# Input projections of a hybrid trunk: three bf16 products in place of one fp32 product, the low halves kept in the weights' own words

## The chip, the cores and the metric

One core of one Trainium2 chip. The metric is the device time of one execution in microseconds (us). The engines of the core are TensorE (PE, matrix products, with a sequencer for weight loads shown as PEld), VectorE (DVE), ScalarE (ACT), GpSimd (POOL) and SyncE (SP), which here issues nearly all DMA transfers. Each engine works through its own list of instructions in order; semaphores hold one back for another.

## What is computed

Two layers of a trunk over 256 latent and 256 context tokens of width 1024. Cut to what matters here:

```python
for layer in range(DEPTH):                      # DEPTH = 2
    h = rmsnorm(x, g) * (1 + m[1]) + m[0]       # latent and context tokens: 512 rows of 1024
    p = h @ w_in[layer]                         # 1024 x 3840, the input projections
    # columns of p: A q,k,v (512 + 256) | B q,i,f_fwd,f_bwd,g (5 x 512) | C q,k,v (512)
    a = diff_attention(p[A]); b = hgrn2(p[B]); c = windowed_attention(p[C])
    x = x + m[2] * (concat(a, b, c) @ w_out[layer])
    x = x + m[5] * ffn(rmsnorm(x) ...)          # layer 0: dense SwiGLU, layer 1: top-2-of-8 experts
```

Inputs, weights and output are fp32. Layer 1 needs no new context tokens, so its queries and gates are computed for the latent tokens alone.

## The kernel before

**Stages.** Per layer: norm of the tokens (into `HT`, 1024 features on 8 x 128 partitions, 512 tokens); input projections; turning of queries and keys (`pe_qkt`); attention (`pe_att`, `act_att`, `dve_att`); the levels of HGRN2 (`pe_levels`), its states, the output projection; then the FFN (layer 0) or the experts (layer 1). The FFN, the output projection and the experts already split each fp32 operand into a bf16 high and low half and add three bf16 products; the input projections multiply fp32 by fp32.

**The projections** (`proj_units`, `pe_proj_mm`) come in eight groups of columns, in this order: `aqk` (queries and keys of A), `c` (all of C), `bff` and `bfb` (the forget gates), `bq`, `av`, `bi`, `bg`. A group has 4 units, a unit is 8 matmuls, one for each block `k` of 128 features, added up in one PSUM bank. For `bff`, `bfb` and `bq` (kind "T") the weights are the stationary operand and up to 512 tokens stream past (in layer 1 `bq` takes 256); for the others (kind "N") 128 tokens are stationary and 512 columns of weights stream (`av` 256). `bg` has 4 units in layer 0 and 2 in layer 1. The trace gives each fp32 matmul as two records.

**The order on PE.** `pe_proj_first` issues the first six groups. In layer 0 pieces of another product (the modulation, `pe_ada_mm`, and its spreading, `pe_ada_spread`, which waits for small copies of the DVE) stand between them. Then `pe_qkt`, the first unit of `bi`, and the attention, between whose steps `pe_proj_fill` puts the other units of `bi` (24 matmuls in layer 0, 16 in layer 1). What is left, `bg` and in layer 1 the last unit of `bi`, is filled into the levels.

**The order on DVE.** `dve_proj_first` copies the units of `aqk` and `c` out of PSUM (L784), then `dve_qk` norms queries and keys (L813 to L832). In its middle GpSimd computes a power (`pool_qk`, L840 and L841), for which the DVE waits (L820); after it GpSimd rotates the latent queries and keys (L855 to L861). In layer 1 16 gate operations (`dve_gates`) follow, which wait for ACT's last sigmoid of `bfb`; in both, the copies of `av`, then those of `pe_qkt` (L1217), then the attention. ACT takes `bff`, `bfb`, `bq`, `bi` and `bg` out of PSUM.

**The attention** runs in steps `s`, one for a head and 128 queries; each passes from PE (scores) to DVE (maximum), ACT (exponential), DVE (ratio), PE (transposes), ACT (copy), PE (product) and DVE (output).

**The weights** are loaded by SP into two rings, R0 and R1, of 16 KiB per partition, groups in turn: `aqk`, `bff`, `bq`, `bi` into R0; `c`, `bfb`, `av`, `bg` into R1. A load starts when PE has done the last unit of the group before in that ring.

```python
def raw_full(eng, key):          # waits until the group's load has landed
    it = items[key]
    eng.wait_ge(S(f"ring_full_{it['place']}"), it["full"])
    return it["raw"]
```

## Time and profile before

| | |
|---|---|
| median of 3 runs | 1839.96 us (1839.65 to 1841.42) |
| the profiled execution | span 1838.2 us from its first to its last instruction; no other time is listed for it |
| PE busy | 1769.7 us (96%), 14950 matmul records |
| DVE busy | 1151.5 us (63%) |
| ACT, POOL busy | 368.6 us (20%), 82.9 us (5%) |
| mean granted clock of TensorE | 0.998 of 2.4 GHz |
| HBM | 221 GB/s over the span; above 400 GB/s in the last third (the experts) |

Such shares don't say where a change pays: they are means over stages with different limits. The rows below are therefore taken from the chain of waits and from the timelines of single stretches. Times in them count from the start of the span. A granted clock of 1.00 is 2.4 GHz, of 0.50 1.2 GHz.

### The profile page before, as it was taken

Reading aid. Unit: us, or ns where it says so; the run is one execution under the profiler, and the core shown is the slowest. Engines: PE = TensorE matmul, PEld = TensorE weight load, DVE = VectorE, ACT = ScalarE, POOL = GpSimd, SP = SyncE. Lnnn points to the kernel's source line nnn. Section 1 sums busy time; section 2 is a strip of 40 time slices with the busy share of each in tenths; the row PEclk is TensorE's granted clock in tenths of the full one; section 3 lists DMA queues with packets and bytes.
Section 4 is the critical chain, followed back from the end, with each engine's and each line's share of the span. In section 5 each row is a group of like instructions: output and inputs, shape, how many; then the busy total and the mean of one; then the engine's idle time right before and its main releaser. Section 6 shows DMA issues by size and latency. Waiting matters only on the chain.

```text
span 1838.2 us, 34033 instructions
## 1 busy us (share of the span) xinstructions
PE 1769.7 (96%) x14950; PEld 1114.3 (61%) x15001; DVE 1151.5 (63%) x1385; ACT 368.6 (20%) x671; POOL 82.9 (5%) x76
## 2 busy tenths in 40 slices
PE   6999999989999999999999978999999999999998
PEld 2434556674544444445465644878696878778695
DVE  1240176896433323214224696999999999999998
ACT  1101155242422222112013432201101010000000
POOL 0033000020000000000330001000000000000000
PEclk9999999999999999999999999999999999999999
DMA  9832200002445454230221017699999999999994
GB/s 371 309 138 69 92 1 29 18 24 98 174 188 206 183 206 160 94 113 3 89 92 69 1 47 281 255 417 409 418 416 415 418 412 419 413 418 410 412 416 194
DMA packets 98842, 408.72 MB, mean 222 GB/s; under 512 B 14008, under 2 KB 20856, under 8 KB 84368
## 3 DMA queue, kind: packets, MB, share of 16 engines
q1 hardware_dynamic: 96504, 405.54, 56.0%
q8 instruction: 119, 1.95, 0.4%
q10 hardware_dynamic: 2200, 1.08, 0.2%
q14 instruction: 19, 0.16, 0.0%
HBM read 405.55 MB, written 1.05 MB: 221 GB/s over the span
## 4 chain that ended last, share of the span: by engine, by line
PE 79%; DVE 10%; DMA 4%; issue 3%; ACT 2%; PEld 1%; ACTq 0%; PEldq 0%; DVEq 0%; SPq 0%; POOL 0%; POOLq 0%
PE PS L1548 12%; PE PS L1924 10%; PE PS L710 9%; PE PS L708 8%; PE PS L1506 6%; PE PS L1898 5%; PE PS L1900 5%; PE PS L1901 5%; DMA ARENA<-in_moe_w 3%; DVE ARENA L2020 2%; PE PS L454 2%; PE PS L1412 2%; PE PS L1274 2%; DVE ARENA L908 2%; DVE ARENA L905 1%
## 5 line engine op out<-in xcount | busy, mean ns | idle before, releaser
L2020 DVE TENSOR_TENSOR ARENA<-ARENA 128x2816 bf16<-128x2816 f32 (+2 forms) x184 | 567.3, 3122 | 23.1 <-DMA ARENA<-in_moe_w 22.6
L1898 PE MATMUL PS<-ARENA 128*128 128x96 bf16 x2816 | 378.6, 209 | 5.8 <-DVE ARENA L2020 3.0
L1900 PE MATMUL PS<-ARENA 128*128 128x96 bf16 x2816 | 378.4, 209 | 1.7 <-issue 1.7
L1901 PE MATMUL PS<-ARENA 128*128 128x96 bf16 x2816 | 378.3, 206 | 0.4 <-issue 0.2
L1900 PEld LDWEIGHTS PS<-ARENA 128*128 128x128 bf16 x2816 | 354.7, 126 | 8.8 <-issue 8.6
L1898 PEld LDWEIGHTS PS<-ARENA 128*128 128x128 bf16 x2816 | 346.3, 123 | 11.8 <-issue 7.5
L1901 PEld LDWEIGHTS PS<-ARENA 128*128 128x128 bf16 x2816 | 298.4, 106 | 2.5 <-issue 2.4
L710 PE MATMUL PS<-ARENA 128*128 128x512 f32 (+1 forms) x608 | 236.9, 530 | 1.3 <-DVE ARENA L623 1.3
L1924 PE MATMUL PS<-ARENA 128*96 128x512 bf16 x960 | 216.1, 384 | 0.4 <-DVE ARENA L2020 0.4
L1548 PE MATMUL PS<-ARENA 128*128 128x512 bf16 x960 | 213.5, 379 | 1.7 <-issue 0.6
L1924 PEld LDWEIGHTS PS<-ARENA 128*96 128x96 bf16 x960 | 116.2, 122 | 93.7 <-issue 0.8
L1548 PEld LDWEIGHTS PS<-ARENA 128*128 128x128 bf16 x984 | 95.0, 98 | 124.8 <-issue 11.7
L710 PEld LDWEIGHTS PS<-ARENA 128*128 128x128 f32 x608 | 109.4, 190 | 85.1 <-issue 79.8
L708 PE MATMUL PS<-ARENA 128*128 128x512 f32 (+1 forms) x384 | 153.7, 559 | 0.0
L387 DVE TENSOR_TENSOR ARENA<-ARENA 128x4096 bf16<-128x4096 f32 (+1 forms) x26 | 91.5, 3519 | 80.9 <-ACT ARENA L381 80.8
L708 PEld LDWEIGHTS PS<-ARENA 128*128 128x128 f32 x384 | 72.2, 190 | 80.7 <-issue 79.1
L1506 PE MATMUL PS<-ARENA 128*128 128x512 bf16 x517 | 113.5, 379 | 1.5 <-DVE ARENA L1600 0.9
L1600 DVE TENSOR_TENSOR ARENA<-PS,ARENA 128x512 f32<-128x512 f32 x22 | 15.2, 692 | 140.7 <-PE PS L1548 140.7
L381 ACT ACTIVATE ARENA<-ARENA 128x4096 bf16<-128x4096 f32 (+1 forms) x26 | 75.1, 2890 | 90.5 <-PE PS L1506 68.3
L1506 PEld LDWEIGHTS PS<-ARENA 128*128 128x128 bf16 x528 | 51.6, 98 | 63.5 <-issue 1.4
L784 DVE COPY ARENA<-PS 128x512 f32<-128x512 f32 (+1 forms) x24 | 13.4, 557 | 107.1 <-PE PS L710 107.1
L1988 ACT ACTIVATE ARENA<-PS 128x384 f32<-128x384 f32 (+1 forms) x48 | 20.7, 465 | 276.1 <-PE PS L1901 275.3
(242 smaller groups left out, 1704.4 us busy)
## 6 DMA issues: line engine op xcount, KB each, us to landing
ARENA<-in_moe_w SPq DMA_DIRECT2D x128, 1408.0 KB, 13.9
ARENA<-in_moe_w SPq DMA_DIRECT2D x48, 1536.0 KB, 16.0
ARENA<-in_ada_w SPq DMA_DIRECT2D x24, 2048.0 KB, 10.1
ARENA<-in_ffn_w SPq DMA_DIRECT2D x15, 2048.0 KB, 7.8
ARENA<-in_w_in SPq DMA_DIRECT2D x11, 2048.0 KB, 7.9
ARENA<-in_moe_w SPq DMA_DIRECT2D x16, 1024.0 KB, 16.0
ARENA<-in_w_in SPq DMA_DIRECT2D x6, 1024.0 KB, 7.0
ARENA<-in_w_out SPq DMA_DIRECT2D x8, 512.0 KB, 4.5
```

The lines of the kernel that those rows point to most:

```text
L381: act.activation(it["hi"], raw, ACT.Copy).then_inc(S("split_hi"), 1)
L387: dve.tensor_tensor(it["lo"], it["raw"], it["hi"], ALU.subtract).then_inc(S("split_lo"), 1)
L454: mm = pe.matmul(ps[32 * g:32 * g + 32, :], SC[:, 2 * kk + n, :], w[:, n, 512 * g:512 * g + 512], start=kk == 0 and n == 0, stop=kk == 3 a ...
L708: mm = pe.matmul(B(bank)[:, part], slot[:, k, P * u:P * u + P], HT[:, k, part], start=k == 0, stop=k == KC - 1)
L710: mm = pe.matmul(B(bank)[:, part], HT[:, k, P * u:P * u + P], slot[:, k, part], start=k == 0, stop=k == KC - 1)
L1506: mm = pe.matmul(B(2 * x + h), a[:, c, P * x:P * x + P], w[:, at:at + 512], start=c == 0 and n == 0, stop=c == FC - 1 and n == 2)
L1548: mm = pe.matmul(B(b0 + i % 3), w[:, k, P * c:P * c + P], x[:, k, :], start=k == 0 and w is hi and x is HTH, stop=k == KC - 1 and w is lo)
L1898: pe.matmul(out, hi[:, h][:, f], HEH[:, k, :], start=k == 0 and b % 4 == 0, stop=False, skip_group_check=True)
L1900: pe.matmul(out, hi[:, h][:, f], HEL[:, k, :], start=False, stop=False, skip_group_check=True)
L1901: mm = pe.matmul(out, lo[:, h][:, f], HEH[:, k, :], start=False, stop=k == KC - 1, skip_group_check=True)
L1924: mm = pe.matmul(B(YBANK + h)[0:SLOTS, :], x, y[:, at:at + 512], start=c == 0 and n == 0, stop=c == FC - 1 and n == 2)
L2020: dve.tensor_tensor(WLO[q % NSLOT][:, 0:n], RAW[q % NSLOT][:, 0:n], WHI[q % NSLOT][:, 0:n], ALU.subtract).then_inc(S("m_lo"), 1)
```

## The change

All groups but `aqk` and `c` are computed as three bf16 products. The high half of an fp32 number is here the upper 16 bits of its word, read in place as bf16 with a step of two elements. The low half of a weight, the number less its high half, rounded to bf16, is written by the DVE over the lower 16 bits of the same word (`dve_proj_halve`), so that no further buffer is needed: one subtraction per group over 8 x 512 elements per partition (8 x 256 for `av`). The tokens' low half goes into a buffer of its own, `HTV` (`dve_tokens_low`), at the place of `G`, whose parts are written when the token tile that lies there has been used for the last time. PE waits for the subtraction of a group (`pe_proj_ready`) and no longer for its load. To make room, ring E1 and the small table `LAMV` move; two step counters of the DVE become one.

```diff
+        HTU = A(0, 2 * KC * 256).bitcast(BF16).rearrange("p (k n two) -> p k n two", k=KC, two=2)[:, :, :, 1]
+        HTV = A(80, KC * 256).bitcast(BF16).rearrange("p (u k t) -> p k u t", k=KC, t=P)
...
+        HALVED = ("bff", "bfb", "bq", "av", "bi", "bg")
+        def word_halves(v):
+            v = v.rearrange("p k n -> p (k n)").bitcast(BF16).rearrange("p (k n two) -> p k n two", k=KC, two=2)
+            return v[:, :, :, 1], v[:, :, :, 0]
...
+        def dve_proj_halve(dve, L, key):
+            raw, w = raw_full(dve, (key, L)), 256 if key == "av" else 512
+            hi, lo = word_halves(raw)
+            dve.tensor_tensor(lo[:, :, 0:w], raw[:, :, 0:w], hi[:, :, 0:w], ALU.subtract).then_inc(S("proj_halved"), 1)
+        def dve_tokens_low(dve, L):
+            dve.wait_ge(S("norm_ht_act"), 16 * L + 8)
+            dve.wait_ge(S("norm_ht_dve"), 16 * L + 8)
+            high, full = (v.rearrange("p k (u t) -> p k u t", t=P) for v in (HTU, HT))
+            dve.tensor_tensor(HTV, full, high, ALU.subtract).then_inc(S("proj_halved"), 1)
+        def pe_proj_ready(pe, L, key):
+            if key not in HALVED:
+                raw_full(pe, (key, L))
+                return
+            pe.wait_ge(S("proj_halved"), proj_halved(L, key))
...
-            if kind == "T":
+            if key in HALVED:
+                hi, lo = word_halves(slot)
+                out = B(bank)[:, part]
+                if kind == "T":
+                    tiles_of = slice(part.start // P, part.stop // P)
+                    terms = [(hi, HTU[:, k, part], out),
+                             (hi, HTV[:, k, tiles_of, :], out.rearrange("p (u t) -> p u t", t=P)),
+                             (lo, HTU[:, k, part], out)]
+                    terms = [(o, w[:, k, P * u:P * u + P], x) for w, x, o in terms]
+                else:
+                    terms = [(out, x, w[:, k, part])
+                             for x, w in ((HTU[:, k, P * u:P * u + P], hi), (HTV[:, k, u, :], hi),
+                                          (HTU[:, k, P * u:P * u + P], lo))]
+                for m, (o, x, y) in enumerate(terms):
+                    mm = pe.matmul(o, x, y, start=k == 0 and m == 0, stop=k == KC - 1 and m == 2)
+            elif kind == "T":
...
                 dve_proj_one(dve, L, n)
+                if n == 3:
+                    dve_tokens_low(dve, L)
+                if n == 5:
+                    dve_proj_halve(dve, L, "bff")
             dve_qk(dve, L)
+            dve_proj_halve(dve, L, "bfb")
+            dve_proj_halve(dve, L, "bq")
             if L > 0:
                 dve_gates(dve, L)
...
+            dve_proj_halve(dve, L, "av")
             for n in range(5 * NT, 6 * NT):
                 dve_proj_one(dve, L, n)
+            dve_proj_halve(dve, L, "bi")
...
             for s in range(len(us) + 4):
+                if s == 6:
+                    dve_proj_halve(dve, L, "bg")
```

The DVE's list around the norm in layer 0, from the copies of `c`'s last two units (L784; L498 and L502 are copies of the modulation) to the first of `pe_qkt`. Before:

```order
L784 COPY ARENA<-PS 128x512
L813 TENSOR_TENSOR ARENA<-ARENA 128x2048
...
L828 TENSOR_TENSOR ARENA<-ARENA,QKG 128x4x256 x2
L832 TENSOR_TENSOR ARENA<-ARENA,SQKG 128x4x256
L832 TENSOR_TENSOR ARENA<-ARENA,SQKG 128x4x128
L502 COPY MT<-PS 128x16
L498 COPY GATE<-PS 128x512 x4
L509 SCALAR_TENSOR_TENSOR MT<-MT,VECS 128x16
L784 COPY ARENA<-PS 128x256 x4
L1217 COPY ARENA<-PS 128x512 x3
```

With the change (L831 is the copy, L720 a group's subtraction):

```order
L831 COPY ARENA<-PS 128x512
L868 TENSOR_TENSOR ARENA<-ARENA 128x2048
...
L887 TENSOR_TENSOR ARENA<-ARENA,SQKG 128x4x128
L720 TENSOR_TENSOR ARENA<-ARENA 128x4096 x2
L505 COPY MT<-PS 128x16
L501 COPY GATE<-PS 128x512 x4
L512 SCALAR_TENSOR_TENSOR MT<-MT,VECS 128x16
L720 TENSOR_TENSOR ARENA<-ARENA 128x8x256
L831 COPY ARENA<-PS 128x256 x4
L720 TENSOR_TENSOR ARENA<-ARENA 128x4096
L1272 COPY ARENA<-PS 128x512 x3
```

The subtractions of `bfb` and `bq` come behind the whole norm, that of `bi` behind the copies of `av` and ahead of those of the turned queries and keys.

In the attention's seventh step, the DVE's list with the change (L1405 ends a step's ratio, L1374 writes an output, L1381 is a maximum):

```order
L1398 RECIPROCAL ARENA<-ARENA 128x2
L1401 TENSOR_SCALAR ARENA<-ARENA,LAM 128x1
L1405 SCALAR_TENSOR_TENSOR ARENA<-ARENA 128x256
L720 TENSOR_TENSOR ARENA<-ARENA 128x4096
L1374 TENSOR_SCALAR ARENA<-PS,ARENA 128x64
L1381 TENSOR_REDUCE ARENA<-PS 128x2
L1384 TENSOR_SCALAR ARENA<-ARENA 128x2
```

There the subtraction of `bg` stands between two steps that before followed each other directly.

## Rows read from the trace of the kernel before

**Rows 1.** The page, the chain that ended last: shares by engine and by line
```profile
PE 79%; DVE 10%; DMA 4%; issue 3%; ACT 2%; PEld 1%; ACTq 0%; PEldq 0%; DVEq 0%; SPq 0%; POOL 0%; POOLq 0%
...
PE PS L1548 12%; PE PS L1924 10%; PE PS L710 9%; PE PS L708 8%; PE PS L1506 6%; PE PS L1898 5%; PE PS L1900 5%; PE PS L1901 5%; DMA ARENA<-in_moe_w 3%; DVE ARENA L2020 2%; PE PS L454 2%; PE PS L1412 2%; PE PS L1274 2%; DVE ARENA L908 2%; DVE ARENA L905 1%
```

**Rows 2.** The chain in order of time: start, length (us), engine, tile, line
```profile
91.14 1.05 PE PS L489 x2
...
109.25 7.06 PE PS L708 x16
...
136.01 34.53 PE PS L708 x80
...
203.89 13.83 PE PS L710 x64
...
221.67 6.87 PE PS L710 x16
...
321.40 1.72 PE PS L710 x4
...
472.56 10.77 PE PS L1480 x96
...
891.86 68.75 PE PS L708 x192
...
960.61 13.83 PE PS L710 x64
...
1047.79 1.72 PE PS L710 x4
```

**Rows 3.** Busy time by stretch, a piece of the FFN in bf16
```profile
core 0: us, PE busy (x) PEld busy (x) DVE busy (x) ACT busy (x) POOL busy (x), PEclk, DMA share, GB/s
506.39:517.13 10.74, 10.74 (x49) 4.88 (x50) 3.60 (x6) 2.82 (x3) 0.00 (x0) 1.00 0.69 280
```

**Rows 4.** Instruction groups, first 760 us: the FFN subtractions on DVE
```profile
L387 DVE TENSOR_TENSOR ARENA<-ARENA 128x4096 bf16<-128x4096 f32 x13 | 57.5, 4422 | 30.4 <-ACT ARENA L381 30.4
...
L387 DVE TENSOR_TENSOR ARENA<-ARENA 128x2048 bf16<-128x2048 f32 x6 | 13.7, 2287 | 1.7 <-ACT ARENA L381 1.6
```

**Rows 5.** Timeline of DVE, both layers: start, length, operation [idle before, releaser]
```profile
86.85 0.69 DVE L784 COPY ARENA<-PS 128x512 f32<-128x512 f32 x1 [8.23 <-PE PS L710]
...
130.57 2.29 DVE L820 TENSOR_TENSOR ARENA<-ARENA,STAT 128x2048 f32<-128x2048 f32 x1 [15.43 <-POOL STAT L841]
...
137.05 1.82 DVE L832 TENSOR_TENSOR ARENA<-ARENA,SQKG 128x1024 f32<-128x1024 f32 x2
...
922.47 1.82 DVE L832 TENSOR_TENSOR ARENA<-ARENA,SQKG 128x1024 f32<-128x1024 f32 x2
```

**Rows 6.** The page, DMA issues of the projections' weights: KB, us to landing
```profile
ARENA<-in_w_in SPq DMA_DIRECT2D x11, 2048.0 KB, 7.9
```

**Rows 7.** Timeline of PE behind two idle times
```profile
22.80 3.14 PE L454 MATMUL PS<-ARENA,SC 128*32 128x512 f32 x16 [3.04 <-DMA ARENA<-in_ada_w]
...
1142.41 1.45 PE L1670 MATMUL PS<-K,ARENA 128*128 128x128 f32 x8 [2.08 <-DVE ARENA L671]
```

**Rows 8.** Busy time by stretch: clock, attention, levels, rotation, gates
```profile
22.80:27.00 4.20, 4.20 (x22) 1.64 (x23) 0.00 (x0) 0.00 (x0) 0.00 (x0) 0.59 1.01 420
...
1142.40:1147.00 4.60, 4.59 (x18) 1.86 (x18) 1.63 (x3) 1.33 (x3) 0.00 (x0) 0.63 1.01 415
...
138.90:153.50 14.60, 14.60 (x35) 6.46 (x34) 0.00 (x0) 2.66 (x5) 13.96 (x16) 1.00 0.41 144
...
228.50:262.20 33.70, 32.85 (x155) 18.40 (x154) 23.76 (x89) 20.09 (x73) 0.00 (x0) 1.00 0.00 0
...
339.50:388.00 48.50, 42.74 (x229) 28.30 (x228) 48.50 (x126) 16.74 (x26) 0.00 (x0) 1.00 0.00 1
...
946.80:960.60 13.80, 13.80 (x65) 12.15 (x65) 6.91 (x16) 3.52 (x6) 0.00 (x0) 1.00 0.24 76
```

**Rows 9.** Instruction groups, first 760 us: weight loads, fp32 and bf16
```profile
L1548 PEld LDWEIGHTS PS<-ARENA 128*128 128x128 bf16 x984 | 95.0, 98 | 124.8 <-issue 11.7 <-DVE ARENA L1600 1.5
...
L710 PEld LDWEIGHTS PS<-ARENA 128*128 128x128 f32 x320 | 57.0, 190 | 53.4 <-issue 51.4 <-ACT ARENA L555 0.2 <-DVE ARENA L623 0.2
```

More of the change, by code:

```diff
@@ L207, in trunk @@
         SQX = [A(108, NT, D), A(93, NT, D), A(93, NT, D), A(20, NT, D)]
-        LAMV = A(68, DEPTH, 4, 32)
+        LAMV = A(128, DEPTH, 4, 32)
         ROWS = A(57, P)
@@ L247, in since @@
             return L * in_layer0[name]
-        RAW_AT = {"R0": A(129, KC, 512), "R1": A(145, KC, 512), "E0": A(40, KC, 512), "E1": A(72, KC, 512),
+        RAW_AT = {"R0": A(129, KC, 512), "R1": A(145, KC, 512), "E0": A(40, KC, 512), "E1": A(64, KC, 512),
                   "E2": A(24, KC, 512),
@@ L400, in trunk @@
         ENG = ("pe", "act", "dve", "pool")
+        dve_steps = [0]
         stage_count = {e: 0 for e in ENG}
@@ L701, in proj_part, with proj_halved @@
             return slice(256, 512) if late else slice(0, 512 if key in ("bff", "bfb", "bq") else w)
+        HALVED = ("bff", "bfb", "bq", "av", "bi", "bg")
+        def word_halves(v):
+            v = v.rearrange("p k n -> p (k n)").bitcast(BF16).rearrange("p (k n two) -> p k n two", k=KC, two=2)
+            return v[:, :, :, 1], v[:, :, :, 0]
+        def proj_halved(L, key):
+            return (len(HALVED) + 1) * L + HALVED.index(key) + 2
+        def dve_proj_halve(dve, L, key):
[12 more added lines that the diff above has]
+            pe.wait_ge(S("proj_halved"), proj_halved(L, key))
         def pe_proj_mm(pe, L, n, k):
@@ L716, in pe_proj_first @@
                 if u == 0 and n + L > 0:
-                    raw_full(pe, (key, L))
+                    pe_proj_ready(pe, L, key)
                 banks = 4 if eng == "act" else 3
@@ L750, in pe_proj_fill @@
                 if key == "bi" and u == 0 or key == "bg" and u == proj_units(L)[-1][1] - (NT if L == 0 else 2) + 1:
-                    raw_full(pe, (key, L))
+                    pe_proj_ready(pe, L, key)
                 if j == 1:
@@ L1708, in dve_route @@
         def dve_route(dve):
-            step = [0]
             def then(ins):
-                step[0] += 1
-                ins.then_inc(S("r_step"), 1)
-                dve.wait_ge(S("r_step"), step[0])
+                dve_steps[0] += 1
+                ins.then_inc(S("dve_step"), 1)
+                dve.wait_ge(S("dve_step"), dve_steps[0])
             def low_rows(j):
@@ L2102, in dve_setup @@
         def dve_setup(dve):
-            step = [0]
             def then(ins):
-                step[0] += 1
-                ins.then_inc(S("setup_step"), 1)
-                dve.wait_ge(S("setup_step"), step[0])
+                dve_steps[0] += 1
+                ins.then_inc(S("dve_step"), 1)
+                dve.wait_ge(S("dve_step"), dve_steps[0])
             dve.wait_ge(S("vecs_copied"), 1)
```

## The prediction

> **What bounds the kernel now.** The page comes first. TensorE (PE) stands for 79% of the chain that ended last, and the projections' two lines, L710 and L708, are 17% of that chain [rows 1]. So the product that the change makes cheaper lies on the path. The chain in order of time then tells where: from 109 us to 229 us in layer 0, and from 892 us to 985 us in layer 1, it consists almost only of projection matmuls, end to end [rows 2]. Next, what a product costs. One fp32 matmul of the program is two records, so 80 records in 34.53 us are 40 matmuls of 0.863 us [rows 2]. A bf16 matmul of 512 columns is read from the FFN: 50 weight loads in 10.74 us, 0.215 us each (49 of the 50 matmul records are there) [rows 3]. At 256 columns it is 13.83 us for 32 fp32 matmuls, 0.432 us each [rows 2], against 96 bf16 ones of the FFN in 10.77 us, 0.112 us each [rows 2].
>
> The DVE's timeline is the last view, since the change gives the DVE seven long subtractions per layer and it works strictly in order. It stands still for 15.43 us in each layer in the middle of the queries' and keys' norm, waiting for GpSimd's power, and only after that does it finish the norm, at 138.9 us in layer 0 and 924.3 us in layer 1 [rows 5].
>
> **The change, step by step.** Three products cost 3 x 0.215 = 0.644 us for 0.863 us: 0.219 us saved per 512-wide matmul, so a unit of 8 takes 5.16 us for 6.91. A 256-wide group of 32 takes 10.8 us for 13.8. If everything stood on the path, layer 0 (160 wide matmuls, 32 narrow) would save 38 us and layer 1 (64 + 32 + 16 = 112 wide, 64 narrow) 31 us. The ceiling is 69 us. The rest of the working says why I take little of it.
>
> A subtraction of 4096 elements per partition takes 4.42 us, one of 2048 elements 2.29 us [rows 4]. The rows are for dense operands; the new ones step over 4 bytes and write half words, which no row shows. I take the dense price, since fp32 words are read in both, and keep twice the price as the far end.
>
> *Layer 0, to the start of attention (228.5 us before).* The tokens' low half fits between two of the DVE's copies, where 8.23 us stood idle [rows 5]. The halving of bff begins behind the copy at 86.85 us (0.69 long) and ends at 92.0; a small copy that followed at once before now comes behind it, and PE, which spread the first gate at 91.1 [rows 2] and must wait for that copy, comes 1.1 us later. Group bff starts at 110.35 and holds three ada chunks, (136.01 - 109.25 - 3 x 7.06) / 3 = 1.86 each: 3 x (7.06 - 1.75) + 3 x 1.86 + 5.16 = 26.7, end at 137.0. But bfb may not start before its own halving, which the program puts behind the whole norm: norm done at 138.9 + 1.1 = 140.0, halving to 144.5. **PE stands still 7.5 us.** Then bfb 20.6, bq 203.9 - 170.5 - 7.0 = 26.4 (its old stretch less the saving), av 10.8. The halvings of bq and av are hidden (bq is loaded 8 us after bff ends [rows 6], and the DVE is free). The halving of bi stands behind av's copies: +0.5, +4.4, and only then bi's first unit, 5.2; the turning of queries and keys (3.25 us) passes beside it. Without clock effects 212.4.
>
> The idle time costs clock. After 3.04 us of idle TensorE was granted 0.59 over 4.2 us, after 2.08 us 0.63 over 4.6 us [rows 7, 8]: most of each stretch at 1.2 GHz in place of 2.4, and 0.41 x 4.2 or 0.37 x 4.6 = 1.7 us of full-rate work lost each time. So the 7.5 us stall brings 1.7 us more: 214.1. **Saved: 14.4 us.**
>
> *Attention, layer 0.* 24 matmuls of bi lie between its steps. In the first 33.7 us PE is busy 32.85 [rows 8], which speaks for all of 24 x 0.219 = 5.3 us; but each step also passes through ACT and DVE in turn, the DVE being busy 23.8 of 33.7, so I take half, 2.6 (ends 0 and 5.3). Against it the halving of bg stands inside this loop at its seventh step. The DVE idles 33.7 - 23.8 = 9.9 us in some 17 steps there, 0.6 us a step, and wins back a part of that: +4.0 of the 4.42. PE then waits over 3 us, and loses clock again; here some of it is covered, +1.5 (ends 0 and 1.7). **Net +2.9.**
>
> *Levels, layer 0.* The first pieces of fill are on the chain, 2 matmuls in 1.72 us and then 2 more [rows 2]: 4 matmuls x 0.219 = **-0.9**. Later the DVE is busy 48.5 of 48.5 us [rows 8], so bg's other 28 matmuls save nothing.
>
> *Layer 1, to the start of attention (985.1 before).* The tokens' half and bff's halving are hidden: the copies there stand 3.5 to 6.9 us apart, a 256-wide unit or a 512-wide one in fp32, and PE has three banks for these units, so a copy that comes 1 us late holds nobody. Group bff runs from 891.9 to 912.5. The norm ends at 924.3, bfb's halving at 928.8: **PE stands still 16.3 us**, over twice what bff had saved, plus 1.7 for the clock. bfb to 951.1, bq (256 wide) to 961.9. The DVE's gates follow bfb and ACT's last two sigmoids (1.2 us): 6.9 us [rows 8], from 952.3 to 959.2; av's halving to 961.5, just in time. av to 972.7, copy and bi's halving to 977.6, bi's unit to 982.9. **Saved: 2.2.**
>
> *Attention and levels, layer 1.* 16 matmuls, 3.5 us at most, I take 2.0; halving of bg +4.0, clock +1.5: **+3.5**. Of the levels three matmuls lie on the chain, 2 of them in the row at 1047.79 [rows 2]: **-0.65**.
>
> What was in step behind each layer keeps its length: the FFN's loads and the experts' weights are started by events that all move together.
>
> Sum: -14.4 + 2.9 - 0.9 - 2.2 + 3.5 - 0.65 = -11.8 us. The profiled span of 1838.2 becomes 1826.4. The median of the runs, 1839.96, lies 1.8 above the span; I add that: **1828.2 us**. About 57 of the 69 us are lost, the larger part to waits for the DVE's halvings.
>
> **A rule that speaks against the change.** During bfb's and bq's halvings GpSimd rotates queries and keys: it was busy 13.96 of 14.6 us right where the DVE did nothing at all (0.00) [rows 8], so no row shows the two at work together. If they take turns at memory, bfb's halving takes up to 8.8 us, 4.4 us more on the path in each layer, and the sum is -3.0. The Trainium skill ("GPSIMD Engine Reference", the table of its properties) says that GpSimd's SBUF interfaces are shared with VectorE, with contention when a DVE instruction has two SBUF inputs, which these have. By that rule the gain would be the 3.0. The trace can't decide it. I keep it as a rival.
>
> **The rivals.**
> - *A: as worked out*, 1828.2. Chance 0.57.
> - *B: the short stalls don't cost clock, or the attention takes up more of the shorter fill.* For it: 2.08 us is the shortest idle time with a fallen clock in the rows, and the attention's stalls may be shorter or covered. Against it: the two long ones are well above. Without all four clock terms 6.4 us less: 1821.8; with all of the fills' 8.8 us in place of 4.6, 1817.6. Chance 0.15.
> - *C: DVE and GpSimd take turns*, 1828.2 + 8.8 = 1837.0, which is 0.16% under before: not to be told from no change, as a measurement of this kernel tells about 0.2%, 3.7 us. Chance 0.15.
> - *D: slower, by weight loads that step over 4 bytes.* The fp32 weight load takes 190 ns, the dense bf16 one 98 [rows 9]. Behind 215 ns of a 512-wide matmul either is hidden; behind the 112 ns of a 256-wide one the longer is not. All 96 products of bq in layer 1 and two of three of av in both layers load from fp32 words: 224 loads. At 190 ns for the 112 of the forecast that is +0.078 x 224 = +17.5 us, 1845.7. It decides against the change from 0.112 + 11.8 / 224 = 0.165 us per load. Against it: an fp32 matmul record of 512 columns lasts 0.43 us, twice a bf16 one, so an fp32 record may hold two rounds, its load too, and 190 be 2 x 95. Chance 0.08.
> - *E: slower, by halvings at twice the price.* Three per layer lie open (bfb, bi, bg), each +4.4: +26.5, 1854.7. Chance 0.05; a read and a write per clock don't depend on the step in any row here, but none has this step.
>
> **The numbers.** The likeliest gives 1828.2. The range, 1818 to 1841, holds A, B and C and the spread of the half-known terms (the fills' 4.2 us below, 3 us of load and queue times above), and leaves out D and E. Faster by over 0.2% are A, B and some of C: 0.76; within 0.2%: most of C, 0.13; slower: D and E, 0.11.
>
> **What would show it.** In the profile after: a 512-wide unit of 24 products in 5.16 us; PE idle 7 to 8 us before bfb in layer 0 and about 16 us in layer 1, both released by the DVE's subtraction; clock near 0.6 behind them; a subtraction of 4.42 us inside attention with PE idle after it; attention starting near 214 and, counted from bff's first matmul of layer 1, 91 us later for 93.3. Subtractions longer than 4.5 us beside GpSimd's rotation mean C, everywhere mean E; 256-wide groups above 12 us mean D. The forecast is wrong in kind if PE doesn't wait before bfb.

## The result: slower by 0.4%, and the profile after

| | before | with the change |
|---|---|---|
| median of 5 runs of each | 1839.96 us (1839.65 to 1842.61) | 1847.57 us (1847.30 to 1849.32) |
| ratio | | 1.0038, 95% interval 1.0025 to 1.0050 |
| profiled span | 1838.2 us | 1845.8 us |
| mean granted clock | 0.998 | 0.981 |

The forecast was 1828.2 us, faster. The time lies above its whole range. TensorE does have less to do, and yet the kernel takes longer. The page of the changed kernel, busy times, granted clock in 40 slices of 46 us, and the chain that ended last:

```profile
PE 1729.5 (94%) x15284; PEld 1096.5 (59%) x15369; DVE 1215.2 (66%) x1399; ACT 368.8 (20%) x671; POOL 101.2 (5%) x76
...
PEclk9999959999999999999989999999999999999999
...
PE 71%; DVE 13%; issue 4%; PEld 4%; DMA 3%; POOL 2%; ACT 1%; PEldq 0%; ACTq 0%; SPq 0%; DVEq 0%; POOLq 0%
```

PE is busy 1729.5 us, where it was 1769.7. The sixth slice, from 231 to 277 us, stands at 5 in the clock row. That is the attention of layer 0, where the forecast saw next to nothing. Against [rows 1] the DVE's share of the chain has grown from 10% to 13%, and PE's has fallen from 79% to 71%.

PE's timeline of the changed kernel at the places that the forecast named (start, length, operation, and in brackets the idle time before it and what ended that):

```profile
111.20 5.27 PE L753 MATMUL PS<-ARENA 128*128 128x512 bf16 x23 [0.17 <-issue]
...
118.25 5.51 PE L753 MATMUL PS<-ARENA 128*128 128x512 bf16 x23
...
145.30 3.59 PE L753 MATMUL PS<-ARENA 128*128 128x512 bf16 x8 [6.95 <-DVE ARENA L720]
...
235.45 1.09 PE L1329 MATMUL PS<-ARENA 128*128 128x64 f32 x4 [3.45 <-DVE ARENA L1374]
...
895.76 21.27 PE L753 MATMUL PS<-ARENA 128*128 128x512 bf16 x94
932.78 2.31 PE L753 MATMUL PS<-ARENA 128*128 128x512 bf16 x5 [15.75 <-DVE ARENA L720]
...
979.34 3.25 PE L1261 MATMUL PS<-K,ARENA 128*128 128x128 f32 x28 [0.61 <-DVE ARENA L831]
984.50 5.34 PE L753 MATMUL PS<-ARENA 128*128 128x512 bf16 x23 [1.91 <-DVE ARENA L720]
989.77 1.13 PE L1299 MATMUL PS<-ARENA 32*128 32x512 f32 x4
...
1013.98 1.94 PE L1329 MATMUL PS<-ARENA 128*128 128x64 f32 x8 [3.61 <-DVE ARENA L1374]
```

From one unit of `bff` to the next, 111.20 to 118.25, is 7.05 us, of which 1.86 are the modulation's piece: a unit takes 5.19 us, as forecast (5.16). PE waits 6.95 us before `bfb` in layer 0 and 15.75 us in layer 1 for a halving (L720); 7.5 and 16.3 were forecast. The wait of 3.45 us inside attention is also there. What is new stands in the clock. Busy time and granted clock by stretch, behind the two waits before `bfb` and then behind the two inside the attentions:

```profile
core 0: us, PE busy (x) PEld busy (x) DVE busy (x) ACT busy (x) POOL busy (x), PEclk, DMA share, GB/s
145.30:149.50 4.20, 3.97 (x9) 1.45 (x11) 2.92 (x1) 0.00 (x0) 4.12 (x4) 0.50 0.05 20
932.70:940.00 7.30, 7.00 (x20) 2.67 (x22) 5.48 (x2) 0.00 (x0) 7.26 (x3) 0.60 0.00 0
235.40:272.00 36.60, 35.88 (x114) 21.98 (x117) 18.57 (x67) 14.00 (x51) 0.00 (x0) 0.50 0.00 1
1013.90:1020.00 6.10, 6.02 (x17) 3.60 (x18) 3.14 (x10) 2.27 (x7) 0.00 (x0) 0.50 0.00 0
```

Behind the long waits in front of `bfb` TensorE is back at 2.4 GHz after 4 to 7 us. Behind the short one of 3.45 us in layer 0's attention it stays at 1.2 GHz for 36.6 us, although it is busy 98% of them. In layer 1, behind a wait of 3.61 us, it is back after some 6 us in this execution.

The DVE's timeline, with [rows 5] for comparison:

```profile
87.67 5.07 DVE L720 TENSOR_TENSOR ARENA<-ARENA 128x4096 bf16<-128x4096 f32 x1
92.59 0.20 DVE L505 COPY MT<-PS 128x16 f32<-128x16 f32 x1
...
140.56 4.68 DVE L720 TENSOR_TENSOR ARENA<-ARENA 128x4096 bf16<-128x4096 f32 x1
...
212.04 1.92 DVE L1272 COPY ARENA<-PS 128x512 f32<-128x512 f32 x3
218.50 0.69 DVE L1381 TENSOR_REDUCE ARENA<-PS 128x2 f32<-128x512 f32 x1 [4.55 <-PE PS L1299]
...
230.13 5.00 DVE L720 TENSOR_TENSOR ARENA<-ARENA 128x4096 bf16<-128x4096 f32 x1
```

A halving of 4096 elements takes 5.0 to 5.1 us and not 4.42 in two of these three rows; the one of `bfb`, with GpSimd's rotation beside it, takes 4.68. And between the copies of the turned queries and keys and the attention's first maximum the DVE stands idle for 4.55 us, 12 us before it is made to do the halving of `bg` in the middle of the attention.

Stage by stage, from the first instruction of one to that of the next (in us; differences are taken before rounding):

| | before | after | difference | forecast |
|---|---|---|---|---|
| start to attention, layer 0 | 228.5 | 217.8 | -10.7 | -14.4 |
| attention, layer 0 | 89.1 | 104.8 | **+15.6** | +2.9 |
| its end to `bff` of layer 1 | 574.1 | 573.2 | -0.9 | -0.9 |
| `bff` to attention, layer 1 | 93.4 | 94.0 | +0.6 | -2.2 |
| attention, layer 1 | 58.1 | 62.7 | +4.7 | +3.5 |
| its end to the end | 795.0 | 793.3 | -1.7 | -0.65 |
| sum | 1838.2 | 1845.8 | +7.6 | -11.8 |

Two thirds of the error of 19.4 us, 12.7 us, lie in one row.

### The profile page after: what moved, and what is told of

Read it like the earlier page. It is cut to its first block, busy times and chain, and to the rows that moved or that the text cites. A ratio compares the mean times of both kernels' runs of the same rounds, so it can differ in the third digit from the quotient of the medians.

```text
span 1845.8 us, 34751 instructions
## 1 busy us (share of the span) xinstructions
PE 1729.5 (94%) x15284; PEld 1096.5 (59%) x15369; DVE 1215.2 (66%) x1399; ACT 368.8 (20%) x671; POOL 101.2 (5%) x76
## 4 chain that ended last, share of the span: by engine, by line
PE 71%; DVE 13%; issue 4%; PEld 4%; DMA 3%; POOL 2%; ACT 1%; PEldq 0%; ACTq 0%; SPq 0%; DVEq 0%; POOLq 0%
PE PS L1605 12%; PE PS L1980 9%; PE PS L753 8%; PE PS L1563 6%; PE PS L1956 5%; PE PS L1954 5%; PE PS L1957 4%; PE PS L757 4%; PE PS L1469 2%; PE PS L1329 2%; PE PS L457 2%; DVE ARENA L720 2%; DVE ARENA L2076 2%; DMA ARENA<-in_moe_w 2%; DVE ARENA L963 2%
## 5 line engine op out<-in xcount | busy, mean ns | idle before, releaser
L1956 PEld LDWEIGHTS PS<-ARENA 128*128 128x128 bf16 x2816 | 354.7, 126 | 8.9 <-issue 8.9
L1954 PEld LDWEIGHTS PS<-ARENA 128*128 128x128 bf16 x2816 | 346.3, 123 | 12.2 <-issue 9.5
L1957 PEld LDWEIGHTS PS<-ARENA 128*128 128x128 bf16 x2816 | 298.5, 106 | 2.3 <-issue 2.2
L753 PE MATMUL PS<-ARENA 128*128 128x512 bf16 (+1 forms) x1068 | 230.2, 365 | 30.1 <-DVE ARENA L720 26.4
L753 PEld LDWEIGHTS PS<-ARENA 128*128 128x128 bf16 x1104 | 106.2, 99 | 140.3 <-DVE ARENA L720 27.6
L1605 PEld LDWEIGHTS PS<-ARENA 128*128 128x128 bf16 x984 | 95.0, 98 | 124.8 <-issue 11.7
L757 PE MATMUL PS<-ARENA 128*128 128x512 f32 (+1 forms) x256 | 99.4, 543 | 1.3 <-DVE ARENA L626 1.3
L1563 PEld LDWEIGHTS PS<-ARENA 128*128 128x128 bf16 x528 | 51.6, 98 | 63.5 <-issue 1.4
L757 PEld LDWEIGHTS PS<-ARENA 128*128 128x128 f32 x256 | 47.6, 190 | 50.2 <-issue 48.1
L1017 PE MATMUL PS<-ARENA 128*128 128x128 f32 x336 | 46.8, 290 | 21.0 <-ACT ARENA L988 14.2
```

The costliest lines, as they stand in the source:

```text
L753: mm = pe.matmul(o, x, y, start=k == 0 and m == 0, stop=k == KC - 1 and m == 2)
L757: mm = pe.matmul(B(bank)[:, part], HT[:, k, P * u:P * u + P], slot[:, k, part], start=k == 0, stop=k == KC - 1)
L1017: mm = pe.matmul(bank[:, c], KEX[:, h, c], crossed_queries(h, x, LEVELS[n_level]), start=True, stop=True)
L1563: mm = pe.matmul(B(2 * x + h), a[:, c, P * x:P * x + P], w[:, at:at + 512], start=c == 0 and n == 0, stop=c == FC - 1 and n == 2)
L1605: mm = pe.matmul(B(b0 + i % 3), w[:, k, P * c:P * c + P], x[:, k, :], start=k == 0 and w is hi and x is HTH, stop=k == KC - 1 and w is lo)
L1954: pe.matmul(out, hi[:, h][:, f], HEH[:, k, :], start=k == 0 and b % 4 == 0, stop=False, skip_group_check=True)
```

## The experiments

All times are medians, and each ratio is to the kernel before, measured beside that kernel on the same chip (1840.4 to 1842.0 us). Where no other kernel is named, a diff is against the change.

**Is it the halving of `bg` inside attention?** Two kernels take it out of its place: one leaves `bg` as one fp32 product, the other puts it 16 steps later in layer 0.

```diff
-        HALVED = ("bff", "bfb", "bq", "av", "bi", "bg")
+        HALVED = ("bff", "bfb", "bq", "av", "bi")
...
-                if s == 6:
-                    dve_proj_halve(dve, L, "bg")
```

> The changed kernel with group bg left in fp32, so that no halving stands inside the attention. Theory 1 (the halving in the attention lets TensorE's clock fall, and in the part with the context's queries it does not come back): the clock stays at 1.00 through both attentions, layer 0's attention takes about 86 us in place of 104, layer 1's about 55 in place of 62; about 0.9 + 0.65 us are given back in the levels. About 23 us less than the change, some 1824 us. Theory 2 (the attention is slow because its fill is now three short bf16 products): attention 0 stays near 100 us and the clock low, 1842 us or more.

Measured: 1824.02 us, ratio 0.991 (0.9893 to 0.9926). The attention takes 86.5 us in layer 0 and 55.8 in layer 1, with the clock at 1.00 in both. So one halving per layer, which saves 1.5 us of fill, costs 23.6 us.

```diff
-                if s == 6:
+                if s == (22 if L == 0 else 6):
```

> The changed kernel with the halving of bg in layer 0 at step 22 of the attention, in the part with the latent tokens' queries, in place of step 6. Theory 1 with the place as a cause (there 512-wide scores keep TensorE busier and the clock comes back within some 5 us, as in layer 1): attention 0 takes about 92 us in place of 104, some 1836 us. If any stall in this attention kept the clock low to its end: 100 us or more, 1845 us.

Measured: 1848.31 us (1839.54 to 1861.32), ratio 1.0035. The wait went along: PE stands still for 3.35 us at 273 us, the clock is 0.50 from there to 297 us, and the attention takes 100.8 us. The place inside the attention does not matter much; that it is inside does. Nor is the 6 us return of layer 1 to be relied on. This kernel has layer 1 as the change has it, and there PE waited 3.46 us; the clock was 0.50 up to 1027 us, and the attention took 68.2 us for 62.7:

```profile
1008.50:1020.00 11.50, 11.49 (x37) 7.43 (x38) 5.14 (x13) 3.87 (x10) 0.00 (x0) 0.50 0.01 1
```

**Is it the wait, or what the wait does to the clock?** Two kernels: the change with 16 useless bf16 matmuls for PE in the wait, and the kernel before with a useless subtraction of the tokens' low half (4.42 us, result not read) in the same seventh step.

```diff
+                    if s == 6:
+                        pe.wait_ge(S("proj_act"), since(L, "proj_act") + 3 * NT + 1)
+                        pe_keep_busy(pe, FILL_BANKS[0], 16)
                     pe.wait_ge(S(n + "at"), since(L, n + "at") + u + 1)
```

> The changed kernel with 16 matmuls without use, 512 columns of bf16 each (3.4 us at full clock), issued by PE in both attentions at the point where it waits for the DVE behind the halving of bg. The stall itself stays. Theory 1: the clock stays at 1.00 behind it, attention 0 falls from 104 us to about 91, attention 1 from 62 to about 60; some 1832 us. Rival (the stall costs by what queues up behind it on the DVE, not by the clock): no change, 1847 us.

Measured: 1845.88 us, ratio 1.0020, but spread from 1830.21 to 1856.98 over ten executions. The profiled one (1835.75) kept the clock at 1.00 in both attentions, and that of layer 0 took 90.7 us. Against the 86.5 us without a halving in it, the wait alone thus costs about 4 us there; the rest of the change's 104.8 us comes with the clock. Over all ten the time goes with the mean clock: 1830.21 us at 0.991, 1844.74 at 0.983, 1856.98 at 0.976. The filler was right where it was looked at, and no cure: what follows a wait in this attention differs from execution to execution.

```diff
+                if s == 6:
+                    high, full = (v.rearrange("p k (u t) -> p k u t", t=P) for v in (HTU, HT))
+                    dve.tensor_tensor(HTV, full, high, ALU.subtract).then_inc(S("stalled"), 1)
```

> The kernel before, with one subtraction without use of 4096 elements (4.42 us) put into the DVE's list at step 6 of both attentions; the products all stay fp32, and with them the fill between the steps. If the stall alone takes the clock down and the context part's small matmuls can't bring it back, whatever the fill: clock 0.50 for over 30 us, attention 0 about 14 us longer, attention 1 about 5 us, 1859 us. If the longer fp32 fill holds the clock or brings it back within 5 us: attention 0 about 5 us longer, 1849 us.

Measured: 1854.02 us, ratio 1.0070 (1.0053 to 1.0087); four executions from 1852.4 to 1854.3 at a mean clock of 0.994 to 0.995, and the profiled one 1874.2 at 0.982. Its two lines of attention in layer 0:

```profile
240.00:250.00 10.00, 7.38 (x30) 4.38 (x29) 8.76 (x21) 3.79 (x16) 0.00 (x0) 0.81 0.00 0
250.00:297.50 47.50, 47.50 (x130) 26.89 (x129) 21.93 (x74) 17.04 (x58) 0.00 (x0) 0.50 0.00 1
```

Not one product was changed here, and a PE wait of 2.62 us was followed by over 47 us at 1.2 GHz with PE busy throughout. So the fall needs no bf16 product. By the mean clocks the long fall came in one execution of five. Whether it is rarer there for the fp32 fills, or for the wait, which is 0.8 us shorter than the change's, these runs don't separate.

**Is it enough to cut the halving up?** At the attention's steps 6, 8, 10 and 12 a quarter of `bg` each, 1.34 us.

```diff
-                if s == 6:
-                    dve_proj_halve(dve, L, "bg")
+                if s in (6, 8, 10, 12):
...
+                    m = KC // len((6, 8, 10, 12))
+                    ks = slice(m * (6, 8, 10, 12).index(s), m * (6, 8, 10, 12).index(s) + m)
+                    ins = dve.tensor_tensor(lo[:, ks, :], raw[:, ks, :], hi[:, ks, :], ALU.subtract)
```

> As the change, but the halving of bg is cut into four pieces of 1.3 us at the attention's steps 6, 8, 10 and 12. Theory 1 (it is the one long subtraction that makes PE wait over 3 us, and only such a wait brings the long stretch at 1.2 GHz): no low clock in attention, 1824.0 (bg in fp32) - 1.5 (bg's first fills in bf16) + 0 to 8 for the DVE's 5 us in each layer = 1822 to 1831. Rival (the 5 us of DVE work inside attention cost the same wherever they stand, or short waits bring the clock down too): 1840 or more.

Measured: 1843.68 us, ratio 1.0007 (0.9997 to 1.0016), and my expectation failed in layer 0. In layer 1 the pieces cost 0.9 us (attention 56.7 us, clock 1.00). In layer 0 PE never waits longer than 0.87 us, and the clock falls all the same:

```profile
230.00:235.00 5.00, 4.24 (x24) 2.41 (x24) 4.75 (x16) 2.93 (x14) 0.00 (x0) 1.00 0.00 0
235.00:240.00 5.00, 4.65 (x21) 3.12 (x21) 3.89 (x12) 3.01 (x11) 0.00 (x0) 0.70 0.00 0
...
237.00:285.00 48.00, 48.00 (x153) 28.56 (x151) 25.86 (x81) 17.04 (x57) 0.00 (x0) 0.50 0.00 1
```

Attention took 106.0 us. Ahead of the fall PE was busy 4.24 of 5 us; with `bg` in fp32 the same stretch shows 4.57. So a few tenths of a microsecond of added idle time stood ahead of this fall. That they are its cause is not shown: the kernel of the next experiment has a stretch with less, at full clock.

**Would another place do?** The DVE's 4.55 idle us ahead of the first maximum:

```diff
-                if s == 6:
+                if s == 0:
                     dve_proj_halve(dve, L, "bg")
```

> As the change, but bg is halved ahead of the attention's first step and not in its seventh: the DVE stood idle there from 213.96 to 218.50 us in layer 0. Theory 1 (the place of this one subtraction makes the 105 us attention): no wait of PE above 1 us inside attention, clock 1.00 there, 86 to 90 us in layer 0 and about 57 in layer 1, so 1845.8 - 17 - 5 = about 1824 for the span, 1826 for the time. In layer 1 the load of bg lands some 1.5 us too late for the first maximum, which the fills cover in part. Rival (bf16 fills between the steps leave PE too little to do to keep the clock, whatever the DVE does): the long low stretch stays, 1840 or more.

Measured: **1823.68 us**, ratio 0.9910 (0.9897 to 0.9923), five executions within 2.2 us. One number in the source is worth 24 us. The DVE, and then PE's least busy 5 us in the first part of layer 0's attention and both attentions:

```profile
214.85 5.10 DVE L720 TENSOR_TENSOR ARENA<-ARENA 128x4096 bf16<-128x4096 f32 x1 [0.57 <-DMA ARENA<-in_w_in]
219.79 0.72 DVE L1381 TENSOR_REDUCE ARENA<-PS 128x2 f32<-128x512 f32 x1
```

```profile
225.00:230.00 5.00, 4.12 (x24) 2.33 (x23) 4.07 (x17) 3.42 (x16) 0.00 (x0) 1.00 0.00 0
...
218.10:304.50 86.40, 82.03 (x473) 50.78 (x473) 61.22 (x193) 49.04 (x150) 0.00 (x0) 1.00 0.00 1
973.20:1029.10 55.90, 53.76 (x306) 33.02 (x305) 37.15 (x97) 30.13 (x77) 0.00 (x0) 1.00 0.00 1
```

In the change the first maximum began 0.74 us behind the first scores, here 1.7 us behind them (218.08), and the fills cover that. This also separates the terms of the forecast. Without wait and clock the attentions take 86.4 and 55.8 us: the cheaper fills save 2.7 and 2.2 us (2.6 and 2.0 forecast). The wait with its clock then cost 104.8 - 86.4 = 18.4 us and 62.7 - 55.8 = 6.9 us.

**What keeps the clock down for 37 us?** In the change, 24 useless dense bf16 matmuls at step 12 of layer 0, in the middle of the low stretch.

```diff
+                if L == 0 and s == 12:
+                    pe.wait_ge(S("proj_act"), since(L, "proj_act") + 3 * NT + 2)
+                    pe_keep_busy(pe, FILL_BANKS[1], 24)
```

> As the change, with 24 useless bf16 matmuls of 128 x 512 at the attention's step 12 of layer 0, in the middle of its long stretch at 1.2 GHz; they take 5.2 us at 2.4 GHz and 10.3 us at 1.2 GHz. Theory 1 (the low clock lasts 37 us because the attention's own mix, products of 32 or 64 rows and of 64 columns, does not bring it back, while dense products do, as behind the waits before bfb): the clock is 1.00 from the burst on, the low stretch ends near 255 in place of 272 us, attention near 100 us, time within 4 us of the change's. Rival (the low stretch lasts its time whatever PE does): the burst is at 1.2 GHz throughout, the stretch ends where it did or later, attention 112 to 115 us, time 1855 or more.

```profile
256.25 6.36 PE L471 MATMUL PS<-K 128*128 128x512 bf16 x24
...
254.00:256.00 2.00, 2.00 (x8) 0.67 (x5) 1.21 (x5) 0.39 (x2) 0.00 (x0) 0.50 0.00 0
256.00:258.00 2.00, 2.00 (x8) 0.83 (x7) 0.03 (x1) 0.91 (x5) 0.00 (x0) 0.50 0.00 0
258.00:260.00 2.00, 2.00 (x10) 0.89 (x9) 0.00 (x0) 0.00 (x0) 0.00 (x0) 0.93 0.00 0
260.00:265.00 5.00, 5.00 (x30) 2.92 (x27) 1.52 (x6) 0.63 (x3) 0.00 (x0) 1.00 0.00 0
```

Two microseconds after the burst begins the clock is back, and it stays at 1.00 to the end of the attention. In the change it came back only after 272 us. So the low stretch did not simply run for its time, and idle time did not keep it up: PE was as busy before the burst (2.00 of 2.00) as in it, and what differed was what it did. In the attention these are products of 32 or 64 rows or of 64 columns and transposes of 128 x 128, with two or three dense ones between. This rests on one profiled execution. The burst's 6.4 us eat up most of what the clock gives back: attention took 103.5 us for 104.8. The time, 1852.64 us, was 5 us above the change's, against the 4 expected at most; by the ratios to the kernel before (1.0054 and 1.0038) it was 3 us. In the profile, whose span is 7 us above the change's, 4.9 us lie between the attention's end and `bff` of layer 1 (578.2 us for 573.2), where nothing was edited; with the 16 filler products it was 577.7. The larger part of it is the clock again. In both kernels it stood at 0.50 for 3.4 us twice on this way, here from 394.8 and from 466.5 us. The first of these falls follows a wait of 2.15 us that the change has too, at the same place and without a fall. With the burst:

```profile
394.33 1.49 PE L1111 MATMUL PS<-K,ARENA 128*128 128x128 f32 x8 [2.15 <-DVE ARENA L966]
```

In the change:

```profile
393.63 1.07 PE L1111 MATMUL PS<-K,ARENA 128*128 128x128 f32 x8 [2.15 <-DVE ARENA L966]
```

So behind the same wait the clock fell in one execution and not in another.

**The waits before `bfb`.** They were forecast rightly, so the halving was moved ahead of the DVE's wait for GpSimd's power (`dve_qk`), where 15.43 us stand idle in each layer.

```diff
                               TMP2[:, :, 0:384].rearrange("p a (g d) -> p a g d", d=64), AX.X, ALU.add).then_inc(S(n + "ss"), 1)
+            dve_proj_halve(dve, L, "bfb")
...
             dve_qk(dve, L)
-            dve_proj_halve(dve, L, "bfb")
```

> As the change, but the halving of bfb stands ahead of the DVE's wait for GpSimd's power (15.4 us of idle time in each layer) instead of behind the whole norm. Theory 1: the bfb stalls are a matter of the order on the DVE alone. Both of PE's waits before bfb go (6.95 us in layer 0, 15.75 us in layer 1) and with each some 2 us of low clock, nothing takes their place: 1847.6 - 6.95 - 15.75 - 4 = about 1821, if the attention of layer 0 keeps its 37 us at 1.2 GHz. Rival: something that these waits hid comes forward (the gates of layer 1, the load of bq), and less than 15 us are won: above 1832. Second rival, on the clock: the long fall in attention comes of the earlier stalls; then it goes too, and the time is near 1805.

Measured: 1837.64 us (1831.46 to 1843.42), ratio 0.9987 (0.9976 to 0.9999), the first rival's side. Both waits are gone, and the long fall in layer 0's attention is not (104.9 us), so it doesn't come of these waits. Layer 0's attention starts 9.6 us earlier, as it should. But the idle time was not free: GpSimd's first operation of the power was held as long as the halving ran, and took 5.01 us for 0.25. The DVE still waited 15.16 us behind its halving, so the norm ended, and the rotation began, some 5 us later than with the old order:

```profile
894.89 5.01 POOL L892 TENSOR_SCALAR STAT<-STAT 128x64 f32<-128x64 f32 x1 [49.84 <-DVE STAT L871]
```

In layer 1 only 7.6 of 17.7 us are won, because of the wait that comes next, before `av`:

```profile
947.78 0.61 PE L753 MATMUL PS<-ARENA 128*128 128x256 bf16 x2 [8.28 <-DVE ARENA L720]
```

My expectation let the 16 gates take 6.9 us. But they now run while GpSimd rotates. The same 16 gates of the change, and of the next kernel (which has the same order there):

```profile
958.10:965.00 6.90, 6.90 (x64) 5.98 (x62) 6.84 (x17) 2.08 (x4) 0.00 (x0) 1.00 0.50 153
```

```profile
916.80:932.30 15.50, 9.64 (x87) 8.10 (x84) 15.44 (x17) 2.84 (x6) 13.84 (x14) 0.92 0.54 172
```

6.84 us of DVE time against 15.44, with POOL busy 13.84 us beside it. The gates, one-input operations, took 0.81 to 1.50 us each while GpSimd worked, and the last two, behind its end, 0.53 and 0.47. GpSimd's operations beside them took about a fifth more than alone (1.66 us for 1.40). So the two hold each other, and here mostly GpSimd the DVE.

**Adding the moves up.** `bfb` as above, `bi` ahead of the third copy of `av`, `bg` in fp32:

```diff
             for n in range(5 * NT, 6 * NT):
+                if n == 5 * NT + 2:
+                    dve_proj_halve(dve, L, "bi")
                 dve_proj_one(dve, L, n)
-            dve_proj_halve(dve, L, "bi")
```

> As the change, with three edits: bfb halved ahead of the wait for GpSimd's power, bi halved ahead of the third copy of av instead of behind the fourth, bg left as one fp32 product. Theory 1 (the costs are the three places of the halvings and the clock behind them, and they add up): 1824.0 (measured with bg in fp32) - 26.7 (both waits before bfb with their clock) - 3.7 (the waits of 1.79 and 1.91 us for bi's halving) = about 1794. Rival (GpSimd or the loads set the end of these stages): above 1805.

Measured: 1807.98 us, ratio 0.9821 (0.9808 to 0.9833); the rival's side. The wait of 8.27 us before `av` accounts for most of the miss. And moving `bi` gained nothing: the turning of queries and keys now waits 3.17 us in layer 0 for the copies that the halving holds back, where `bi`'s unit had waited 1.6.

The same two moves with `bg` in quarters:

> All six groups as three products: bfb halved ahead of the wait for GpSimd's power, bi ahead of the third copy of av, bg in four pieces at the attention's steps 6, 8, 10 and 12. Theory 1: the time of the kernel with bg in fp32 and the same two moves (about 1794) - 1.5 + 0 to 8, so 1792 to 1801. Rival (the pieces cost clock): 1812 or more. If it stands above the kernel with bg in fp32, then bg's three products are worth less than the DVE's 5 us.

Measured: 1820.95 us (1811.67 to 1832.06), ratio 0.9893 (0.9859 to 0.9928), the rival's side: the fall of the clock again (attention of layer 0 100.5 us), in some executions more than in others.

**All subtractions moved.** `av` in layer 1 between the tenth and eleventh gate operation, `bi` in two halves of which PE waits for one at a time, and `bg` at the attention's front; and the same with `bg` in fp32.

```diff
             for d in range(2):
                 for h in range(NH):
+                    if (d, h) == (1, 1):
+                        dve_proj_halve(dve, L, "av")
...
+            for ks in (slice(0, KC // 2), slice(KC // 2, KC)):
+                dve.tensor_tensor(lo[:, ks, :], raw[:, ks, :], hi[:, ks, :], ALU.subtract).then_inc(S("proj_halved"), 1)
...
+            if j == 0 and k == KC // 2:
+                pe.wait_ge(S("proj_halved"), proj_halved(L, "bi") + 1)
```

> All six groups as three products, four subtractions moved: bfb ahead of the wait for GpSimd's power, av in layer 1 between the tenth and the eleventh gate operation, bi in two halves of which PE waits for one at a time, bg ahead of the attention's first step. Theory 1 (every wait of PE before a group was one of order on the DVE): waits of PE above 1 us before attention gone in both layers, clock 1.00 from bff to the levels; 1824.0 (bg in fp32, rest as in the change) - 9 and - 17.7 (bfb with its clock) - 3.3 (bi) + about 1 for bg = 1795. Rival (GpSimd's rotation and the gates, which slow each other, keep the end of av where it was in layer 1; the attention of layer 0 falls to 1.2 GHz again in some executions): 1805 to 1820.

Measured: 1817.33 us (1805.02 to 1829.22), ratio 0.9860 (0.9814 to 0.9905), and my 1795 failed. Three executions at 1805 to 1808 with a mean clock of 0.993 to 0.994, three at 1827 to 1829 with 0.978 to 0.979. The profiled one is of the second kind: PE waits 2.02 us at 213 us, the clock is 0.50 from 215.4 to 273.5 us, and the attention takes 111.2 us. The DVE now waits for the load of `bg`, since the attention starts earlier and the load does not:

```profile
206.35 5.07 DVE L720 TENSOR_TENSOR ARENA<-ARENA 128x4096 bf16<-128x4096 f32 x1 [2.02 <-DMA ARENA<-in_w_in]
```

> As the kernel before it in this call, but bg left as one fp32 product, without its halving. Theory 1: 1824.0 - 9 - 17.7 - 3.3 = 1794, and within 2 us of the kernel with bg in three products: bg's saving in fills (1.5 us) and its halving (0 to 2 us) cancel. Rival (three products of bg gain in the levels too, or its halving costs clock): more than 4 us between the two, in favour of bf16 in the first case and of fp32 in the second.

Measured: 1798.95 us, ratio 0.9769 (0.9757 to 0.9782), five executions within 3.5 us. From `bff` on no wait above 1 us is left in front of layer 0's attention; in layer 1 4.07 us are left before `av`.

The last two: all six groups as three products with `bi` in one piece, so that the attention starts later (2.0 us in the profiles) and the load of `bg` lands in time (the DVE waits 0.67 us for it in place of 2.02), `av` behind eight gate operations; and the kernel of 1798.95 us with `av` moved alike.

> All six groups as three products; bfb halved ahead of the wait for GpSimd's power, av in layer 1 behind eight gate operations, bg ahead of the attention's first step, bi in one piece as in the change. Theory 1 (the kernel with bi in two pieces fell to 1.2 GHz in half of its executions because attention then began 1.6 us earlier, while bg's load and halving did not, which made the wait of 2.02 us): no wait above 1 us inside attention, clock 1.00 there in every execution, 1823.7 (bg ahead of attention) - 9.6 - 17.7 + 1.2 (what is left before av) = 1797.6. Rival (bf16 bg with bfb moved is on the brink whatever the place): executions at 1805 to 1830 again, clock .98 to .99.

Measured: **1798.43 us**, ratio 0.9769 (0.9755 to 0.9783), 1796.51 to 1801.97. Attentions of 86.4 and 55.8 us at a clock of 1.00. It is the change itself with three subtractions in other places, and 49 us faster than it.

> As the fastest so far (bg in fp32, bfb ahead of GpSimd's power, bi in two pieces), with av's halving of layer 1 behind eight gate operations in place of ten. The wait of 4.07 us before av falls by these two operations' 2.9 us to 1.2 us, and with it the clock's 1.7 us: 1799.0 - 2.9 - 1.7 = 1794.4. Rival (the load of av lands later and sets the wait): 1797 to 1799.

Measured: 1797.76 us, ratio 0.9759 (0.9745 to 0.9772), which can't be told from the last. The wait before `av` fell to 2.10 us and not to 1.2, since the halving itself now takes 3.65 us beside GpSimd's rotation (2.64 us alone):

```profile
920.87 3.65 DVE L720 TENSOR_TENSOR ARENA<-ARENA 128x2048 bf16<-128x2048 f32 x1
```

**The price of a halving.** In the kernel before, four useless subtractions of 2048 elements in the DVE's idle time of layer 1, written in turn densely and with a step of two half words.

> The kernel before, with four useless subtractions of 2048 elements per partition in the DVE's idle 15 us of layer 1 (result never read): tokens less their high halves, written in turn densely and with a step of two half words, none over its own operand. Theory 1 (the write of single half words costs 15%): 2.29 us for the dense ones, 2.6 us for the stepped ones. Rival (the price comes of writing into the words that the same instruction reads): 2.29 us for all four.

One line's durations, minimum, median and maximum:

```profile
L827 DVE TENSOR_TENSOR ARENA<-ARENA x4: 2282/2430/2569, 901.9 to 909.1; 128x2048 bf16<-128x2048 f32 x4
```

In their order they took 2.28, 2.57, 2.29 and 2.57 us, dense and stepped in turn, and none writes over its own operand. So the stepped half-word write costs 13%, and most of the change's 15% (5.07 for 4.42 us) is due to it.

## Why the prediction was wrong, point by point

- **Prices.** The unit of 5.16 us was right (5.19), and the waits before `bfb` too (7.5 and 16.3 forecast, 6.95 and 15.75 found). Rival D fell: the weight loads of L753 from fp32 words take 99 ns on average. That its 1845.7 us lies next to the measured 1847.57 is chance. Rival E fell, but "I take the dense price" was low by 15%.
- **Start to attention, layer 0** ("saved: 14.4 us", found 10.7). 0.8 us were lost by the start of `bfb` (145.3 for 144.5), of which 0.6 by the norm's end (140.6 for 140.0) and 0.3 by the halving's 4.68 us; and 1.0 at `bi`, mostly its halving's 5.11 us in place of 4.42. The 1.9 us between, from `bfb` to the end of `av`, are partly clock: it was 0.50 to 149 us and 0.83 to 152, some 2.4 us of full-rate work for the 1.7 forecast. The rest I can't assign.
- **The step that failed** is "PE then waits over 3 us, and loses clock again; here some of it is covered, +1.5 (ends 0 and 1.7)". Wait and fills were right: 3.45 us and -2.7. The clock's part is 18.4 - 3.45, about 15 us, where the upper end was 1.7. That end came from two rows of 4.2 and 4.6 us [rows 8], in which PE worked on products over all 128 rows, of 512 and of 128 columns [rows 7]. The attention of layer 0 is another mix, and no row of the kernel before showed it at a low clock at all. By the method that I used, bounds from the nearest rows, the far end should have been the whole rest of the attention at half rate. No rival gave the clock more, either. That the halving's place makes the wait and the fall is shown by its move to the front (18.4 us back, nothing else edited), and the kernel before with an added subtraction shows that the fall doesn't need the change's products. That the mix of products keeps the clock down so long rests on the one burst; why the length differs between executions stays open.
- **`bff` to attention, layer 1** (-2.2, found +0.6). From `bfb`'s start to attention it took 57.0 us for 54.1: 0.8 for `bi`'s halving and its start, clock 2.9 us instead of 1.7 (0.50 to 935, 0.65 to 940), and 0.9 over many products, unassigned.
- **Attention, layer 1** (+3.5, found +4.7). Wait and clock cost 6.9 us for the 5.5 forecast. The term was right in kind, and the small miss partly luck: with the same layer 1, the kernel with `bg` later in layer 0 lost another 5.5 us here. Rival B's first half fell with both attentions: behind both waits the clock was 0.50.
- **Rival C**, DVE and GpSimd in turns, was right in kind and had the wrong victim in mind. Of the halvings beside the rotation, `bfb`'s took 4.68 us in layer 0, and the two of layer 1 10.14 together, no more than alone. Only `bq`'s in layer 0, begun 0.16 us behind a GpSimd operation, took 5.98, and it was off the path. Mostly GpSimd was held: its first two rotations took 1.40 us before.

```profile
928.20 10.52 POOL L910 TENSOR_TENSOR ARENA<-ARENA,K 128x256 f32<-128x256 f32 x2 [8.41 <-DVE ARENA L887]
```

  By the rule of the Trainium skill that the prediction cited ("GPSIMD Engine Reference", Specifications) there is contention with DVE instructions that have two SBUF inputs or run in a mode of two ports. The trace agrees for the first, and adds which side paid: mostly GpSimd, which began behind the DVE. The gates have one SBUF tensor input; whether they ran in such a mode no row tells. POOL's time was not on the path, so the forecast lost nothing by it. It came on the path in the experiments, through the gates.
- **The chances** don't add up as written: D and E together are 0.13, not 0.11, and what is left of C within 0.2% is 0.11, not 0.13. And the range's lower end, 1818, leaves out the 1817.6 us of rival B that it is said to hold. Neither changes the account.
- **What was not asked.** The forecast asked of each halving what it delays. It never asked of `bg`'s whether the DVE had idle time a few steps before, though the 8 us of loading and the end of `av` put the data there in time.

## What to carry to other kernels

A short wait of PE is priced by what PE does behind it. With dense products the clock was back in 2 to 7 us; in the first part of layer 0's attention, a mix of few-row and few-column products, it stayed at half rate for 34 to 58 us, and in the later parts, with scores of 512 columns, for 7 to 24 us. So where such a mix is the stage, put long operations of its feeding engines ahead of it, where those stand idle, and rely on no slack inside. When a wait is taken away, compute the next one with the neighbours that the shift creates: the gates took over twice their time once they ran beside GpSimd.

## What the runs showed of the hardware that I had not expected

- TensorE was granted 0.50 for 36.6 us with PE busy 98% of them, in the kernel before with one added subtraction for 47.5 us with PE busy all of them, and with all subtractions moved for 58.1. A burst of dense bf16 products of 6.4 us was followed by full clock about 2 us from its start.
- Whether the clock falls, and for how long, differed between executions of one kernel: 1805 or 1828 us, with mean clocks of 0.993 and 0.978. The two kernels that varied most spread over 24 and 27 us, the kernel before beside them over 5.5 and 5.6 us. Behind one and the same wait of 2.15 us the clock fell in one profile and not in another.
- Half words written with a step of two: 2.57 us for 2.28 at 2048 elements.
- DVE beside GpSimd: in a two-input subtraction GpSimd was held (10.52 us for 1.40, 5.01 for 0.25), in one-input fp32 operations mostly the DVE (15.44 us for 6.84). A halving begun behind a GpSimd operation was held itself (5.98 us for 5.07, 3.65 for 2.64).
